# Gate product from one float32 copy, compressed scores block-diagonal, leftovers of tile 1 behind the output of tile 0, first query panel in halves

## The chip, the cores and the metric

The kernel runs on one core of one Trainium2 chip. The metric is the device time of one execution in microseconds (us), the median of several runs; lower is better. TensorE is PE in the profile, VectorE DVE, ScalarE ACT, GpSimd POOL and SyncE SP.

## What is computed

Four transformer layers on 256 tokens of width 1024, all in float32. The change touches the third layer (native sparse attention, NSA) and the router of its expert layer.

```
proj = x @ w_in
gates = jax.nn.sigmoid(proj[..., ATTN_WIDTH + 6 * kvd:])   # 48 columns
k_cmp = compress_blocks(rope(kv[:, :, 0]), ...)            # 15 blocks of 32 tokens per group
p_c = masked_softmax(q @ k_cmp, cmp_end <= t)              # compressed branch
# selected and window branches: ordinary causal attention at 256 tokens
out = gate0 * o_c + gate1 * o_s + gate2 * o_w              # then @ w_out, + h, rms_norm
```

16 heads of 64 share 4 groups of keys. The expert layer takes, for each token, 8 heads of 256 query columns; each half of a head's query (128 columns) is scored against 128 keys, the 16 best of each half give 256 sums, and the 16 best of these name 16 of 16384 experts. With 8 x 16 = 128 experts a token it forms `h = gelu(u[e] . x)` and adds `gate * h * v[e]`. The fourth layer is forgetful attention and another such expert layer.

## The kernel before, in words

Tokens lie on the 128 partitions in two tiles (0 and 1). Matrices come as panels of 2 MB (1024 x 512) through a ring of two slots; SyncE issues their loads.

**Front, 0 to 840 us.** Two layers and the wide NSA product. Here a float32 product is done as three fp32r products: ScalarE casts a high part of each panel (`ring_hi`), VectorE forms the rest (`ring_lo`), and the transposed tokens have the same two parts (`xT`, `xT_lo`). `evict_turned` (ScalarE) copies the transposed tokens out of PSUM banks 4 to 7, VectorE's `lower_turned` subtracts. After the last wide panel, `narrow` (line 686) multiplies the tokens by the 48 gate columns: for each tile, each of 8 slices and each of the two parts one float32 matmul, with the tokens as weights.

**Middle, from 840 us.** `MIDDLE` is an order written out by hand. Each name is one step that fills one PSUM bank, on six rotating banks; PE runs the names in order, and ScalarE or VectorE (`by_dve`) empties each bank in the same order. A and B are transposes of the queries of tiles 0 and 1, T and D and E of key twins (D1, E1 those of tile 1), H the compression's hidden product (four panels), G and C its further steps, c0 and c1 the compressed scores (line 1006), X and e0 to e3 the compressed values (e2, e3 for tile 1), S, P, O the scores, the turned shares and the values of one batch of four heads of tile 0; o turns the mixed result and u0, u1 multiply it by the output matrix. Names with ! fill no bank (!E exponentials of a batch, !m !x !n the compressed softmax). For c0 and c1, each of 16 (tile, head pair) has one matmul on the 64 rows of one head with 16 columns; c0 does the first heads of the pairs, c1 the second.

After u1, VectorE adds both halves to h and runs `norm_late` (ScalarE's `root` gives the square root); xn of tile 0 is then ready.

**route00.** The router of tile 0, also in order: y0, y1 turn xn; w0 to w3 multiply it by the four query panels (`project_late`, line 872), W turns four blocks of 128 query columns, s scores them against the keys (line 895). ScalarE copies each result. One panel holds two heads. VectorE ranks head 0 (`rank_head`), then `choose` writes the experts of piece 0 (head 0 alone), then it computes the gates of the piece, for which it waits for ScalarE's exponentials (g0, after s1 in ScalarE's order), then it ranks head 1, and only then does it begin the expert slots.

**Expert stream, to the end.** 4 windows of 128 slots. GpSimd gathers, for each slot, 128 rows of u and of v (0.52 MB each, line 2118), four u slots ahead of four v slots, in rings of eight rows; it waits for a free slot (`u_used`, `v_used`). VectorE forms the dot with u (line 1757), ScalarE the gate and a diagonal matrix, PE adds diagonal x v into PSUM (line 852). Four slots are one tick, and between ticks each engine runs the steps of NSA tile 1, of the routers and of the last layer that are due (`STAGES`).

Of the kernel before, what the change touches and what calls it, by code (L numbers as in the profile page):

```python
# [17 lines left out]
F32 = mybir.dt.float32  # L18
# [6 lines left out]
P = 128  # L25
SEQ = 256
# [48 lines left out]
def in_batch(kind, t, b):  # L75
# [11 lines left out]
          ["G2", "c0", "c1", "S4a", "S4b", "P3a", "O2", "!m", "!E4", "!x", "G3"],  # L87
# [3 lines left out]
          ["P7a", "O6", "D1", "E1"],  # L91
          ["O7", "e2", "e3"],
          ["o0", "o1"], ["u0", "u1"]]
# [12 lines left out]
def fox_plan(t):  # L106
    plan = [(1, ["x0", "x1"]), (2, ["f", "q0"]), (3, ["q1", "Q0"]), (4, ["c", "k0", "Q1"]),
            (5, ["k1", "K0"]), (6, ["v0", "K1"]), (7, ["v1"])]
    for i in range(BATCHES + 2):
# [10 lines left out]
          ("route00", -1, [(0, ["y0", "y1", "w0", "W0", "s0", "w1", "w2", "W1", "s1", "w3", "W2", "s2", "W3", "s3"])]),  # L120
# [12 lines left out]
WEIGHTS = {"w": 0, "q": 0, "k": 2, "v": 4, "u": 6}  # L133
USES = [key for key in ORDER if key[1][0] in WEIGHTS or key[1][0] == "H"]
# [153 lines left out]
def build(nc, x, panels, gains, consts, line_consts, rel_bias, lam, subln, small, fbias, keys, u0, v0, u1, v1, out,  # L288
          probe=None):
    lines_dram = nc.dram_tensor("bias_lines", (HEADS, P, LINE), F32).ap()  # L290
    with ExitStack() as ctx:
# [93 lines left out]
        kcT = z(GROUPS, CW)  # L385
# [44 lines left out]
        tokT = o[:, 1, :].rearrange("p (a b) -> p a b", a=KT)  # L430
        turned_q = [o[:, 1, :].rearrange("p (a b) -> p a b", a=PAIRS),
# [53 lines left out]
        gate_logits = sem("gate_logits")  # L485
        gate_exps_ready = sem("gate_exps_ready")
# [93 lines left out]
        @block.sync  # L580
        def _(sp):
            sp.dma_start(h[:, :, :], x.rearrange("(t p) d -> p t d", p=P)).then_inc(first_loaded, 16)

            sp.wait_ge(first_loaded, 16 * 5)
            for s in range(2):
                if s == 1:
                    sp.wait_ge(landed[0], 16)
                sp.dma_start(ring[:, s, :], panels[s]).then_inc(landed[s], 16)
            pairs = N_PANELS // 2
            with sp.Fori(1, pairs) as i:  # L590
                for s in range(2):

                    sp.wait_ge(panel_used, i * 2 + (s - 1))
                    sp.dma_start(ring[:, s, :], panels[i * 2 + s]).then_inc(landed[s], 16)
            for n in range(2 * pairs, N_PANELS):
                sp.wait_ge(panel_used, n - 1)
                sp.dma_start(ring[:, n % 2, :], panels[n]).then_inc(landed[n % 2], 16)
            for i, key in enumerate(USES):
                n = N_PANELS + i
                if i < 2:  # L600
                    sp.wait_ge(panel_used, n - 1)
                else:
                    filled(sp, USES[i - 2])
# [8 lines left out]
        def _(pe):  # L612
# [68 lines left out]
            def narrow(w, cols):  # L681

                for t in range(TILES):
# [191 lines left out]
            def route(stage, layer, t, begin, plan):  # L875
                for tick, names in plan:
                    yield begin + tick
                    for name in names:
                        key = stage, name
                        if name[0] == "y":  # L880
                            pe.wait_ge(xn_ready, NORM_NUMBER[("nsa", "ffn1")[layer], t])
                            turn_half(key, xn[:, t, :])
                        elif name[0] == "w":
                            emptied(pe, (stage, "y1"))
                            project_late(key)
                        elif name[0] == "W":
                            i = int(name[1])
                            turn_projected(key, wqT[:, 4 * i:4 * i + 4, :])
                        else:
                            i = int(name[1])  # L890
                            emptied(pe, (stage, f"W{i}"))
                            pe.wait_ge(keys_landed, 16 * (TILES * layer + t + 1))
                            to = bank(key)
                            for j in range(4):
                                last = mm(to[:, j * P:(j + 1) * P], wqT[:, 4 * i + j, :], keysT[:, 4 * i + j, :],
                                          start=True, stop=True)
                            last.then_inc(bank_filled, 1)
# [56 lines left out]
            def middle(stage, begin, plan):  # L954
                pe.wait_ge(proj_read, 2 * AHEAD + 2 * done)
                for tick, names in plan:
                    yield begin + tick
                    for name in names:
# [40 lines left out]
                        elif kind == "c":  # L999
                            emptied(pe, (stage, "B1"))  # L1000
                            emptied(pe, (stage, "C0"))
                            to, own = bank(key), slice(i * HD, (i + 1) * HD)
# [124 lines left out]
        def _(act):  # L1127
# [17 lines left out]
            def evict_turned(call):  # L1145
# [4 lines left out]
                for t in range(TILES):  # L1150
# [4 lines left out]
                    if t == 0:  # L1155
                        upper(first, 0, steps=range(early, CHUNKS))

# [137 lines left out]
            def route(stage, layer, t, begin, plan):  # L1295
                moments = [(begin + tick + (begin + tick >= 0), names) for tick, names in plan]
                if stage == "route00":
                    names = plan[0][1]
                    moments = [(begin, names[:9] + ["g0"] + names[9:])]
                moments += [(chosen_at(stage, begin, piece), [f"g{piece}"])  # L1300
                            for piece in range(stage == "route00", len(CHOSEN[TILES * layer + t]))]
                for tick, names in sorted(moments, key=lambda m: m[0]):
                    yield tick
                    for name in names:
# [6 lines left out]
                        if name[0] == "y":  # L1311
                            copy_bank(key, tokT[:, 4 * i:4 * i + 4, :], fours(key))
                        elif name[0] in "wW":
# [28 lines left out]
            def middle(stage, begin, plan):  # L1342
# [28 lines left out]
                root()  # L1371
# [102 lines left out]
        def _(dve):  # L1474
# [312 lines left out]
            def route(stage, layer, t, begin, plan):  # L1787
                window = TILES * layer + t
                for head in range(P_HEADS):
                    yield ranked_at(stage, begin, head)  # L1790
                    emptied(dve, (stage, f"s{head // 2}"))
# [79 lines left out]
            def middle(stage, begin, plan):  # L1871
# [3 lines left out]
                v.memset(hidT, 0.0)  # L1875
                dve.wait_ge(gate_exps_ready, 1)
# [4 lines left out]
                for tick, names in plan:  # L1881
                    yield begin + tick
                    for name in names:
# [20 lines left out]
                        elif name == "C0":  # L1904
                            filled(dve, key)
                            v.tensor_copy(kcT, shadow_bank(key)[:, 0:GROUPS * CW].rearrange("p (a b) -> p a b", a=GROUPS))\
                                .then_inc(dve_emptied, 1)
# [9 lines left out]
                        elif kind == "c":  # L1917
                            filled(dve, key)
                            for t in range(TILES):
                                last = v.scalar_tensor_tensor(  # L1920
                                    out=over(cmp_s[:, t, i, :], [[2 * CW, PAIRS], [1, CW]]),
                                    in0=over(shadow_bank(key)[:, t * PAIRS * CW:], [[CW, PAIRS], [1, CW]]), scalar=SCALE,
                                    in1=over(const("cbias")[:, t * CW:(t + 1) * CW], [[0, PAIRS], [1, CW]]),
                                    op0=ALU.mult, op1=ALU.add)
# [21 lines left out]
                dve.drain()  # L1946
                norm_late(0, "ffn0", xn_ready)
# [287 lines left out]
```

## Time and profile before

| What | us |
|---|---|
| median of 3 runs | 2611.57 (2604.69 to 2615.46) |
| the profiled execution | 2603.34 |
| its span in the trace | 2601.2 |
| PE busy | 2196.6 (84%) |
| VectorE busy | 1408.9 (54%) |
| GpSimd busy | 1139.3 (44%) |
| ScalarE busy | 873.8 (34%) |

### The profile page before, as it was taken

How to read it: one execution, taken by the hardware profiler on the slowest of the kernel's cores; microseconds unless marked ns; L12 is line 12 of the kernel's file. 1: busy time of each engine (PE TensorE's matmuls, PEld its weight loads, DVE VectorE, ACT ScalarE, POOL GpSimd, SP SyncE). 2: the span in 40 equal slices, each digit the busy share in tenths (PEclk: the TensorE clock that was granted, in tenths of full speed). 3: DMA queues.
4: the chain of work that ended last, by engine and by line, in shares of the span. 5: the costliest groups of instructions: out<-in, count | busy, mean ns of one | idle time of the engine just before them, and what ended most of it. 6: DMA issues, size and time to landing. Idle time of an engine off the chain costs nothing.

```text
span 2601.2 us, 24135 instructions
## 1 busy us (share of the span) xinstructions
PE 2196.6 (84%) x7346; PEld 1283.3 (49%) x7346; DVE 1408.9 (54%) x2912; ACT 873.8 (34%) x2112; POOL 1139.3 (44%) x1075
## 2 busy tenths in 40 slices
PE   5879999889989987688896989798899897767767
PEld 4656876668868743254342444343345343323222
DVE  2365445364457347855565654465665457664433
ACT  2344443444533423254222324222235222222121
POOL 0000000000000006667666757667666767777674
PEclk8899999899999888888998999898999998888888
DMA  8504544225444339889999999999999999999997
GB/s 229 190 25 153 194 182 150 105 81 190 174 168 151 148 114 390 321 306 333 414 414 381 368 412 371 391 413 407 372 414 348 404 412 359 355 372 380 363 369 282
DMA packets 165575, 754.64 MB, mean 290 GB/s; under 512 B 18320, under 2 KB 18464, under 8 KB 152544
## 3 DMA queue, kind: packets, MB, share of 16 engines
q0 software_dynamic: 149168, 544.02, 55.1%
q1 hardware_dynamic: 13952, 197.14, 19.6%
q10 hardware_dynamic: 2352, 12.24, 1.2%
q8 instruction: 48, 0.79, 0.1%
q14 instruction: 55, 0.45, 0.0%
HBM read 749.13 MB, written 4.19 MB: 290 GB/s over the span
## 4 chain that ended last, share of the span: by engine, by line
PE 37%; DVE 15%; POOL 12%; issue 10%; DMA 9%; another core or an unknown queue 6%; ACT 3%; DVEq 1%; ACTq 0%; POOLq 0%; SPq 0%
POOL Z L2118 12%; PE ps L852 9%; DMA Z<-v,experts 6%; PE ps L639 6%; PE ps L641 6%; PE ps L640 6%; DVE Z L1757 6%; PE ps L872 3%; DMA Z<-u,experts 2%; PE ps L978 1%; PE ps L913 1%; DMA ring<-panels 1%; PE ps L904 1%; DVE ring_lo L1606 1%
## 5 line engine op out<-in xcount | busy, mean ns | idle before, releaser
L852 PE MATMUL ps<-Z 128*128 128x512 f32 x2048 | 1014.7, 652 | 254.0 <-DMA Z<-v,experts 174.3
L852 PEld LDWEIGHTS ps<-Z 128*128 128x128 f32 x2048 | 416.6, 209 | 814.9 <-issue 569.3
L1757 DVE CUSTOM_DVE_ANT_0 Z<-Z,xn 128x1024 f32<-128x1024 f32 x512 | 609.2, 1224 | 297.8 <-DMA Z<-u,experts 235.0
L2118 POOL DMA_INDIRECT Z<-u,experts x512 | 571.5, 1116 | 388.8 <-issue 161.2
L2118 POOL DMA_INDIRECT Z<-v,experts x512 | 543.8, 1062 | 219.8 <-issue 134.3
L1606 DVE TENSOR_TENSOR ring_lo<-ring,ring_hi 128x1024 fp32r<-128x1024 f32 x212 | 246.0, 1219 | 274.8 <-ACT ring_hi L1142 274.8
L639 PE MATMUL ps<-ring_hi,xT_lo 128*128 128x512 f32 x592 | 238.1, 402 | 32.5 <-DVE xT_lo L1654 17.8
L872 PE MATMUL ps<-ring,o 128*128 128x512 f32 x576 | 255.0, 596 | 1.9 <-ACT o L1278 1.4
L1142 ACT CAST ring_hi<-ring 128x1024 fp32r<-128x1024 f32 x212 | 206.9, 1049 | 129.2 <-DMA ring<-panels 119.6
L641 PE MATMUL ps<-ring_hi,xT 128*128 128x512 f32 x592 | 232.9, 393 | 0.0
L640 PE MATMUL ps<-ring_lo,xT 128*128 128x512 f32 x592 | 232.9, 393 | 0.0
L1259 ACT ACTIVATE hdot<-hdot 128x4 f32<-128x4 f32 x128 | 26.4, 206 | 557.7 <-DVE hdot L1757 389.6
L2107 POOL COPY Z<-pj 128x256 f32 x16 | 6.4, 400 | 434.3 <-ACTq L526 343.3
L1270 ACT ACTIVATE Z<-cst,wslot 128x128 f32<-128x128 f32 x512 | 164.7, 390 | 66.7 <-remote 29.0
L872 PEld LDWEIGHTS ps<-ring,o 128*128 128x128 f32 x576 | 108.8, 191 | 133.6 <-issue 131.6
L2150 POOL COPY ksc<-pj 128x512 f32<-128x512 f32 x5 | 3.4, 710 | 332.5 <-DVE pj L1676 319.3
L639 PEld LDWEIGHTS ps<-ring_hi,xT_lo 128*128 128x128 f32 x592 | 113.0, 191 | 62.5 <-DVE ring_lo L1606 16.0
L640 PEld LDWEIGHTS ps<-ring_lo,xT 128*128 128x128 f32 x592 | 113.0, 191 | 24.0 <-issue 1.2
L641 PEld LDWEIGHTS ps<-ring_hi,xT 128*128 128x128 f32 x592 | 112.5, 190 | 24.1
L1264 ACT ACTIVATE wslot<-hdot,gate_w 128x1 f32<-128x1 f32 x512 | 109.6, 284 | 9.1 <-issue 0.3
L639 PE MATMUL ps<-ring_hi,hT 128*128 128x512 f32 x256 | 101.2, 395 | 5.3 <-DVE hT L1614 5.3
L1278 ACT COPY scratch<-ps 128x512 f32<-128x512 f32 x68 | 38.0, 577 | 189.4 <-PE ps L872 71.9
(257 smaller groups left out, 2067.1 us busy)
## 6 DMA issues: line engine op xcount, KB each, us to landing
ring<-panels SPq DMA_DIRECT2D x93, 2048.0 KB
Z<-u,experts POOLq DMA_INDIRECT x512
Z<-v,experts POOLq DMA_INDIRECT x512
gain<-gains ACTq DMA_DIRECT2D x4, 1024.0 KB, 7.7
pj<-keys ACTq DMA_DIRECT2D x4, 1024.0 KB
bias_lines<-xn POOLq DMA_DIRECT2D x1, 3072.0 KB, 38.5
gain<-gains ACTq DMA_DIRECT2D x5, 512.0 KB, 6.2
Z<-bias_lines POOLq DMA_DIRECT2D x1, 2048.0 KB, 9.5
```

The source lines that it names most:

```text
L639: mm(out, b, c, start=start, stop=False)
L640: mm(out, a, d, start=False, stop=False)
L641: return mm(out, a, c, start=False, stop=stop)
L852: last = mm(ps[:, c, :], diag[s], vrow[s][:, c * NC:(c + 1) * NC], start=slot == 0, stop=slot == SLOTS - 1)
L872: last = mm(to, tokT[:, k, :], w[:, k * NC:(k + 1) * NC], start=k == 0, stop=k == KT - 1)
L1142: copy(ring_hi[:, slot, c * CH:(c + 1) * CH], ring[:, slot, c * CH:(c + 1) * CH]).then_inc(hi_ready, 1)
L1264: f(own[:, s:s + 1], cols[:, s:s + 1], ACT.Copy, scale=gate_w[:, t, slot + s:slot + s + 1])
L1270: f(diag[n % RING], ident, ACT.Copy, scale=own[:, s:s + 1]).then_inc(diag_ready, 1)
L1278: copy(to, src).then_inc(act_emptied, 1)
L1606: v.tensor_tensor(ring_lo[:, slot, at], ring[:, slot, at], ring_hi[:, slot, at].bitcast(F32), ALU.subtract).then_inc(lo_ready, 1)
L1757: v.tensor_tensor_reduce(out=urow[s], in0=urow[s], in1=xn[:, t, :], scale=1.0, scalar=0.0, op0=ALU.mult, op1=ALU.add, accum_out=hdot[:, t, ...
L2118: g.indirect_dma_start(out=rows[s], out_offset=None, in_=tables[layer], in_offset=bass.IndirectOffsetOnAxis(ap=experts[:, t, slot:slot + 1 ...
```

## The change

Four edits.

1. `evict_turned` copies, before the NSA product, all transposed tokens once more out of PSUM as plain float32 (`xT_all`, in the place of `o`, four copies of 128x512); `narrow` waits for them and does one matmul per tile and slice instead of two.
2. The compressed keys are stored block-diagonal (`kcT` gets a second half, cleared by a memset; C0 copies two quadrants). c0 does both heads of a pair in one matmul over all 128 rows with 32 columns; c1 is gone, and VectorE reads 256 elements a tile at once.
3. e2, e3, D1 and E1 (tile 1) move behind u0, u1 and the norm of tile 0, which now has a name of its own, !r.
4. In route00, w0, W0 and s0 become i0, j0, t0 (head 0: 256 columns, two transposes, two score products) and i1, j1, t1 (head 1). Both use the one panel; the slot is given free after i1. VectorE waits for t0 and t1.

```diff
           ["H3", "S3a", "S3b", "P2a", "O1", "!E3"],
-          ["G2", "c0", "c1", "S4a", "S4b", "P3a", "O2", "!m", "!E4", "!x", "G3"],
+          ["G2", "c0", "S4a", "S4b", "P3a", "O2", "!m", "!E4", "!x", "G3"],
...
-          ["P7a", "O6", "D1", "E1"],
-          ["O7", "e2", "e3"],
-          ["o0", "o1"], ["u0", "u1"]]
+          ["P7a", "O6"], ["O7"],
+          ["o0", "o1"], ["u0", "u1", "!r"], ["e2", "e3", "D1", "E1"]]
...
-          ("route00", -1, [(0, ["y0", "y1", "w0", "W0", "s0", "w1", "w2", "W1", "s1", "w3", "W2", "s2", "W3", "s3"])]),
+          ("route00", -1, [(0, ["y0", "y1", "i0", "j0", "t0", "i1", "j1", "t1", "w1", "w2", "W1", "s1", "w3", "W2", "s2", "W3", "s3"])]),
...
-USES = [key for key in ORDER if key[1][0] in WEIGHTS or key[1][0] == "H"]
+USES = [key for key in ORDER if key[1][0] in "wqkvuH" or key[1] == "i0"]
+LAST_USE = {("route00", "i0"): ("route00", "i1")}
...
-                        for n, a in enumerate(tokens(k, t)):
-                            last = mm(ps[:, 4 + t, 0:cols], a.bitcast(F32), w[:, k * cols:(k + 1) * cols],
-                                      start=k == 0 and n == 0, stop=k == KT - 1 and n == 1)
+                        last = mm(ps[:, 4 + t, 0:cols], xT_all[:, k, t * P:(t + 1) * P], w[:, k * cols:(k + 1) * cols],
+                                  start=k == 0, stop=k == KT - 1)
...
+                        elif name[0] == "i":
+                            emptied(pe, (stage, "y1"))
+                            w, b, to = late_panel((stage, "i0")), int(name[1]), bank(key)
+                            for k in range(KT):
+                                at = k * NC + b * NC // 2
+                                last = mm(to[:, 0:NC // 2], tokT[:, k, :], w[:, at:at + NC // 2], start=k == 0, stop=k == KT - 1)
+                            last.then_inc(bank_filled, 1)
+                        elif name[0] == "j":
+                            b = int(name[1])
+                            emptied(pe, (stage, f"i{b}"))
+                            to = bank(key)
+                            for j in range(2):
+                                last = tr(to[:, j * P:(j + 1) * P], wqT[:, 2 * b + j, :], ident)
+                            last.then_inc(bank_filled, 1)
...
-                                    at = (t * PAIRS + pair) * CW
-                                    last = mm(to[:, at:at + CW], turned_q[t][own, pair, :], kcT[own, pair // 2, :],
+                                    at = (t * PAIRS + pair) * 2 * CW
+                                    last = mm(to[:, at:at + 2 * CW], turned_q[t][:, pair, :], kcT[:, pair // 2, :, :],
...
+                if NEXT[call] == "nsa":
+                    act.wait_ge(xt_ready, 2 * TILES * (call + 1))
+                    for t in range(TILES):
+                        for b in range(2):
+                            last = copy(xT_all[:, 4 * b:4 * b + 4, t * P:(t + 1) * P],
+                                        ps[:, 4 + 2 * t + b, :].rearrange("p (a b) -> p a b", a=4))
+                    last.then_inc(xt_all_ready, 1)
...
+                v.memset(kcT, 0.0)
```

## Rows read from the trace of the kernel before

**Rows 1.** windows: stretch, length, busy us by engine, PE clock, DMA share, GB/s

```profile
979.90:2575.61 1595.71, 1317.74 (x3362) 606.64 (x3360) 938.12 (x2227) 473.32 (x1471) 1111.69 (x1021) 0.91 0.98 378
...
996.84:1077.00 80.16, 57.56 (x119) 25.09 (x119) 69.76 (x229) 22.19 (x70) 61.48 (x55) 0.82 1.02 406
```

**Rows 2.** timeline of GpSimd: start, length, what, idle before and its releaser

```profile
979.90 1.02 POOL L2118 DMA_INDIRECT Z<-u,experts  x1 [123.64 <-DVE experts L1730]
...
998.85 1.18 POOL L2118 DMA_INDIRECT Z<-u,experts  x1 [4.22 <-DVE hdot L1757]
...
1083.65 1.18 POOL L2118 DMA_INDIRECT Z<-u,experts  x1 [5.61 <-DVE hdot L1757]
```

**Rows 3.** timeline of VectorE, first rank, gate norm, first dot

```profile
969.50 0.49 DVE L1682 MAX8 ranks<-ksc 128x8 f32<-128x128 f32 x2 [15.44 <-ACT ksc L1278]
...
987.08 0.17 DVE L1743 TENSOR_REDUCE ranks<-ranks 128x1 f32<-128x16 f32 x1 [7.14 <-ACT ranks L1293]
...
996.84 1.23 DVE L1757 CUSTOM_DVE_ANT_0 Z<-Z,xn 128x1024 f32<-128x1024 f32 x1 [1.25 <-issue]
```

**Rows 4.** timeline of ScalarE, copy of s1

```profile
984.94 0.59 ACT L1278 COPY ksc<-ps 128x512 f32<-128x512 f32 x1 [1.25 <-PE ps L895]
```

**Rows 5.** windows of the gate product alone (line 686)

```profile
840.15:844.10 3.95, 3.95 (x37) 3.95 (x36) 1.00 0.69 218
...
844.75:849.80 5.05, 5.05 (x25) 5.05 (x25) 0.50 0.72 296
```

**Rows 6.** chain of waits, by time: start, length, what

```profile
850.07 5.76 PE ps L951 x32
...
855.83 7.02 PE ps L978 x32
...
871.77 0.87 PE ps L951 x8
...
909.67 1.12 PE ps L904 x4
...
910.78 1.61 PE ps L913 x8
```

**Rows 7.** timeline of VectorE, last memset and the adds of T0 to T3

```profile
845.32 0.17 DVE L1875 MEMSET Z<- 128x128 f32 x1
...
852.70 5.39 DVE L1889 TENSOR_TENSOR Z<-ps,smallw 64x480 f32<-64x480 f32 x8 [1.27 <-PE ps L951]
```

**Rows 8.** timeline of ScalarE and VectorE, split of the second NSA panel

```profile
790.53 3.91 ACT L1142 CAST ring_hi<-ring 128x1024 fp32r<-128x1024 f32 x4
...
791.63 4.63 DVE L1606 TENSOR_TENSOR ring_lo<-ring,ring_hi 128x1024 fp32r<-128x1024 f32 x4 [0.63 <-ACT ring_hi L1142]
...
796.98 0.59 ACT L1168 COPY pj<-ps 128x512 f32 x1 [2.54 <-PE ps L641]
```

**Rows 9.** windows of the compressed scores alone (line 1006)

```profile
892.76:895.50 2.74, 2.74 (x25) 2.74 (x25) 1.00 0.99 425
...
896.95:902.20 5.25, 5.25 (x28) 5.25 (x28) 0.50 0.01 3
```

**Rows 10.** timeline of VectorE, adds of O6 and O7

```profile
929.95 0.18 DVE L1825 RECIPROCAL shares<-totals 128x4 f32<-128x4 f32 x1 [1.60 <-PE ps L913]
...
932.16 0.86 DVE L1837 SCALAR_TENSOR_TENSOR o<-ps,shares,o 128x64 f32<-128x64 f32 x4
```

**Rows 11.** timeline of PE: y0 and y1, w0, w1 and w2

```profile
954.11 1.97 PE L859 MATMUL ps<-cst,xn 128*128 128x128 f32 x8 [5.10 <-DVE xn L1783]
...
956.76 8.91 PE L872 MATMUL ps<-ring,o 128*128 128x512 f32 x16 [0.68 <-ACT o L1278]
...
968.68 13.90 PE L872 MATMUL ps<-ring,o 128*128 128x512 f32 x32
```

**Rows 12.** timeline of SyncE, load of the panel for w3

```profile
975.74 0.33 SPq L604 DMA_DIRECT2D ring<-panels  x1
```

**Rows 13.** windows, a stretch of the first attention

```profile
158.00:160.00 2.00, 0.39 (x1) 0.30 (x2) 1.70 (x4) 0.36 (x1) 0.00 (x0) 1.00 0.00 0
```

More of the change, by code:

```diff
@@ L384, in build @@
         cmp_s = z(TILES, HEADS, CW)
-        kcT = z(GROUPS, CW)
+        kcT = z(GROUPS, 2, CW)
         bd = z(2, 8, HD)
@@ L602, in _ @@
                 else:
-                    filled(sp, USES[i - 2])
+                    filled(sp, LAST_USE.get(USES[i - 2], USES[i - 2]))
                 sp.dma_start(ring[:, n % 2, :], panels[panel_source(key)]).then_inc(landed[n % 2], 16)
@@ L889, in route @@
                         else:
-                            i = int(name[1])
-                            emptied(pe, (stage, f"W{i}"))
+                            i, blocks, turned = int(name[1]), *((2, "j") if name[0] == "t" else (4, "W"))
+                            emptied(pe, (stage, f"{turned}{i}"))
                             pe.wait_ge(keys_landed, 16 * (TILES * layer + t + 1))
                             to = bank(key)
-                            for j in range(4):
-                                last = mm(to[:, j * P:(j + 1) * P], wqT[:, 4 * i + j, :], keysT[:, 4 * i + j, :],
+                            for j in range(blocks):
+                                last = mm(to[:, j * P:(j + 1) * P], wqT[:, blocks * i + j, :], keysT[:, blocks * i + j, :],
                                           start=True, stop=True)
@@ L1312, in route @@
                             copy_bank(key, tokT[:, 4 * i:4 * i + 4, :], fours(key))
+                        elif name[0] in "ijt":
+                            to = (ksc if name[0] == "t" else wqT)[:, 2 * i:2 * i + 2, :]
+                            copy_bank(key, to, fours(key)[:, 0:2, :])
                         elif name[0] in "wW":
@@ L1370, in middle @@
                             soft_exps(stage, int(name[2]))
-                root()
+                        elif name == "!r":
+                            root()
             def nsa(stage, begin, plan):
@@ L1790, in route @@
                     yield ranked_at(stage, begin, head)
-                    emptied(dve, (stage, f"s{head // 2}"))
+                    emptied(dve, (stage, f"t{head}" if stage == "route00" and head < 2 else f"s{head // 2}"))
                     rank_head(head, ksc[:, 2 * head:2 * head + 2, :])
@@ L1905, in middle @@
                             filled(dve, key)
-                            v.tensor_copy(kcT, shadow_bank(key)[:, 0:GROUPS * CW].rearrange("p (a b) -> p a b", a=GROUPS))\
-                                .then_inc(dve_emptied, 1)
+                            for m in range(2):
+                                own = slice(m * HD, (m + 1) * HD)
+                                last = v.tensor_copy(kcT[own, :, m, :], shadow_bank(key)[own, 0:GROUPS * CW]
+                                                     .rearrange("p (a b) -> p a b", a=GROUPS))
+                            last.then_inc(dve_emptied, 1)
                         elif name == "C1":
@@ L1920, in middle @@
                                 last = v.scalar_tensor_tensor(
[L1921 to L1923 removed]
+                                    out=cmp_s[:, t], in0=over(shadow_bank(key)[:, t * HEADS * CW:], [[CW, HEADS], [1, CW]]),
+                                    scalar=SCALE,
+                                    in1=over(const("cbias")[:, t * CW:(t + 1) * CW], [[0, HEADS], [1, CW]]),
                                     op0=ALU.mult, op1=ALU.add)
```

15 lines of the change are left out of this document (10 added, 5 removed).

## The prediction

> **What bounds the kernel now.** I read the page's forty slices and queue table first, then windows from the first gather on, then GpSimd's timeline, then the chain of waits through the stretch before it. From 980 us on the kernel streams expert rows, and everything else lies beside that: the DMA engines are 0.98 busy over 1596 us [rows 1]. Their bytes don't change, so the end comes earlier only as far as the stream starts earlier. When does it really start? GpSimd issues its first gather at 979.90, twelve in all (eight u, four v), and stands until VectorE's first dot frees a u slot [rows 2]. That dot runs at 996.84. VectorE had ranked head 0 from 969.50, then sat 7.14 us for the gate exponentials of piece 0, and ranked head 1 [rows 3]. The exponentials were late because ScalarE runs them in order behind the copy of s1, which ended at 985.5 [rows 4]. From 996.84 to 1077 VectorE is busy 69.8 of 80.2 us, and at 1083.65 GpSimd waits on it for 5.6 us [rows 1, 2]: VectorE's clock from the first dot, not the first gather, sets the pace. So I follow what moves the first dot: the chain 840 to 955 (PE almost throughout), then route00.
>
> **Gate product.** Each float32 matmul appears as two records in the trace (the product's 32 matmuls are 64 records). After: 16 matmuls, 32 records. The rate was 3.95/36 = 0.11 us a record at the full clock and 5.05/25 = 0.20 once the granted clock had fallen to half (1.2 GHz) at 844.3 [rows 5]. 32 x 0.11 = 3.5 us, so the product ends near 843.8 instead of 850.07: 6.3 us. The 32 transposes behind it took 5.76 us, largely at half clock; eight of B0 and B1 took 0.87 at the full one, so 3.5 for 32 [rows 6]. They would end at 847.3, but H0 needs T0 from VectorE. That engine ends its memsets at 845.5, gets one more (0.17, the size of the last of them), then adds and inverts the gates (about 1.1 with its waits) and does T0's two adds (2 x 5.39/8 = 1.35): 848.2 [rows 7]. H0 began at 855.8, so the gain is 7.5, with VectorE late next. If the clock falls all the same behind the product, the transposes keep 5.76: 849.5, gain 6.3. If everything runs at half clock, 32 x 0.20 + 5.76 leaves 3. I take 7.5: the clock fell 4.15 us into the product, and this one lasts 3.5.
>
> The price is ScalarE's four copies (128x512, 0.55 us each, 2.2) before the dense product, behind VectorE's last xT_lo at 791.0. They hold back the split of the second panel: ScalarE began it at 790.53 and VectorE its first quarter at 791.63; now 793.8 and 794.9, first quarter done at 796.1. PE wants it when the first panel is through, just before 796.98 [rows 8]. Hidden by 0.4 us; if that cover is gone it costs up to 1. TensorE's new wait is satisfied 40 us early.
>
> **Compressed scores.** c0 and c1 were 32 matmuls of 16 columns on 64 rows: 64 records, 892.8 to 902.3, 2.74 us for 25 at full clock and 5.25 for 28 at half [rows 9]. Now 16 matmuls of 32 columns on 128 rows, 32 records. No row has that shape; the nearest, 48 columns on 128 rows, costs 0.11 [rows 5], the half-clock price 0.20. So 3.5 to 6.5 us against 9.5: gain 6.0 down to 3.0. I take 3.5. Behind it runs a loop of transposes, values, VectorE's add, ScalarE's exponentials: at half clock 1.1 and 1.6 on PE [rows 6], and about 0.95 and 1.7 on the two others, a period of some 5.4 us. In the likeliest case it stays at half clock (these columns are narrower than the gate's, and waits follow), and the gain is 6.2 with small waits saved. If the clock stays up, P (four transposes, half of 0.87, and 0.15 for the way out) and O (8 records of 0.11) are together some 1.2 us shorter: 1.8 until P4a, then 0.9, 0.1 (there VectorE is the bound, with the compressed softmax) and 1.1 in the further rounds, together 9.9 with the 6.0. VectorE's reads of the product keep their elements, and the second kcT copy (0.2) lies 9 us before its use.
>
> **Leftovers.** e2, e3 (4 records of 13.90/32 = 0.43 [rows 11], 1.75) and D1, E1 (0.87) leave the stretch between P7a and o0. Not all of it is gained: O7 moves up by D1's and E1's 0.87, but VectorE's adds for O6, from 929.95, and for O7 follow each other in 1.35 each; they then end at 932.65, where they ended at 933.02 [rows 10]. Gain 0.4; 0 if the share copy for O7 is late, and 2.6 would be the whole of it. They land behind u1, where PE idled 5.10 us for the norm [rows 11]: 2.6 of work hides in it. ScalarE's two copies (1.1) come behind the root and before y0. VectorE's copies of e2 and e3 come behind the norm, where it waited 15.44 us [rows 3]; i0 and j0 take their banks, and the copies are through a little before i0. If they were not, i0 would wait up to 0.7.
> That leaves 2.5 us of idle PE where 5.1 had been. After 5.1 the clock was at half: y0 and y1 took 1.97 and w0 8.91 against 13.90 for two panels [rows 11]. Kept at full, y0 and y1 are 0.9 to 1.0 shorter: 0.9; 0 if the clock falls.
>
> **Query panel in halves.** Before: w0 8.91 us, then copy, W0, copy, s0, copy; head 0 ranked at w0's start + 12.7, first gather at + 23.1. After: i0 is 16 records of 256 columns; H0's 32 of that width took 7.02 [rows 6], so 3.5. Then copies of half the width (0.35), two transposes (0.3), two score matmuls (0.6): with releases 2.3 instead of 3.8. Head 0 starts at + 5.8, first gather + 16.3: 6.9 us earlier relative to the panel. But VectorE blocks at the gate norm until ScalarE has passed s1. Until there PE has i0, j0, t0 5.3, i1, j1, t1 5.3, w1 and w2 14.0 (13.90 before), W1 and s1, so s1's copy ends at + 27.6 where it was + 28.8. The exponentials follow by 1.5 and the first dot 9.8 after them: + 39.0 instead of + 40.1 [rows 3, 4, 11]. So this edit moves the first gather by 6.9 and the first dot by 1.1. The stretch between is a longer wait on VectorE, about 13 us instead of 7.14. The panel for w2 is issued when i1 is filled, + 8.9, as before when w0 was; the one for w3 when w1 is filled, now behind the first gathers; before, at 975.74, ahead of them [rows 12]. If the clock falls before i0 as it did before w0, i0 takes 1.8 more and this term is -0.7.
>
> **Sum.** 7.5 + 6.2 + 0.4 + 0.9 + 1.1 = 16.1 us, first dot at 980.7, and the stream behind it is rigid. The profiled execution took 2603.3 (span 2601.2); 2587.2 for it. It lies 8.2 under the median shown, 2611.57; I set the change against the median: 2595.5, say 2596.
>
> **A rule of the Trainium skill.** TensorE's clock rose again at about 854.6, inside a run of nothing but transposes that had begun at 850.07 [rows 5, 6]. The Trainium skill's page "TensorE: Matmul & The Clock Gate", Part 4 (PE-mode transpose), says that transposes don't count as busy time for the clock. By that, the transposes behind the gate product would lower the clock rather than hold it, and the gate term would be 6.3, the sum 14.9. The row speaks against the rule; I give it weight only within rival B.
>
> **Rivals.** Those on the clock differ in where it falls.
> A. It stays up through the scores too: gate 7.5, scores 9.9, rest 2.4: 19.8, time 2592. For it: in the first attention, with the same mixture of small transposes and products, PE was busy only 0.39 of 2 us in one stretch and the clock stayed 1.00 [rows 13]. Against: it had fallen 2.7 us into the old scores, with PE busy throughout.
> B. It falls at the old places and also before i0: 6.3 + 4.5 (between 3.0 and 6.0) + 0.4, y as before, and i0 some 1.8 longer, which leaves -0.7 there: 10.5, time 2601. For it: the clock fell 4.15 and 2.7 us into the narrow products, and neither new one is much shorter. The transpose rule of the Trainium skill pulls this way.
> C. The head start carries: DMA is full from 980 on [rows 1], so twelve gathers served 6.9 - 1.1 = 5.8 us sooner would shorten the end as well: 16.1 + 5.8 = 21.9, time 2590. Against: only eight u slots exist, the twelve (12 x 0.524 MB at 406 GB/s) take 15.5 us, and then DMA has nothing until the first dot.
> D. The other side: w3's panel starves. It is issued 1.4 us after the first gather, behind 12 x 0.52 MB; before, it was issued 4.2 us ahead of it [rows 2, 12]. PE, in order, stands at w3, ScalarE behind it can't make a diag, v slots don't come free and GpSimd stops. In fair sharing it lands at + 30, 3 us late, without effect. It costs from + 43 on, us for us: w3 7, W3 and s3 3, gates and diags 3, first v slot 2 make + 58, and GpSimd restarts at + 41 with twelve gathers, some 17 us, before it asks for a v slot; from + 59 it eats all 16 us, and if gathers keep it back until their second round of eight is in (another 11 us a round), the kernel is slower than before, 2615 to 2630. Against: later panels are issued in the full stream and the stream goes on.
> E. The change does not do what it says: the stream re-times itself and swallows the gain, its clock being 0.91 on average, 0.82 at first [rows 1]: 2606 to 2614.
>
> **Chances.** Forecast 0.45 (own range 11 to 21 us less: 2591 to 2601), A 0.17, B 0.19, C 0.07, D 0.05, E 0.07. About 0.5% (13 us, below 2598.5) can be told from no change. Faster: 0.45 x 0.75 + 0.17 x 0.95 + 0.19 x 0.25 + 0.07 = 0.61; slower: most of D, 0.04; same 0.35. The range takes in A, B and C and part of E, and runs of before are spread over 11 us: 2585 to 2609.
>
> **What would show it.** Product over 32 records of 0.11 and H0 near 848; c0 near 885 over 3.5 us; u0 near 921; e2 to E1 right behind u1; first gather near 958, then a wait of some 13 us on VectorE and the first dot near 981; DMA share below 1 between them. Wrong if the first dot moves by under 10 us, if the stream from first dot to end (1604 us) lengthens, or if PE waits for the second panel of the dense product.

## The result

The changed kernel takes 2580.89 us (median of 13 runs, 2575.39 to 2594.56); the kernel before, run beside it, took 2597.62 (13 runs, 2576.61 to 2615.46). The ratio is 0.9941, 95% interval [0.9919, 0.9964]: 0.6% faster. The difference was forecast at 16.1 us and came out at 16.7 by the medians, 15.3 by the ratio. The absolute time was forecast at 2596 and lies 15 us lower, below the range (2585): it had been set on a median of 2611.57, and the same kernel then gave 2597.62.

Where the time came from is seen in the profile of the changed kernel. Its windows show the gate product alone (the answer to [rows 5]; PE and weight load busy, clock, DMA share, GB/s):

```profile
837.40:842.00 4.60, 3.67 (x32) 3.56 (x32) 1.00 0.74 241
```

32 records instead of 64, all at 1.00. The timeline of PE, from there to route00 (answers to [rows 6, 9, 11]):

```profile
837.47 3.67 PE L688 MATMUL ps<-smallw,o 128*128 128x48 f32 x32
840.97 1.06 PE L967 MATMUL ps<-cst,pj 128*128 128x128 f32 x8
841.86 1.91 PE L967 MATMUL ps<-cst,ksc 128*128 128x128 f32 x16
843.61 1.04 PE L967 MATMUL ps<-cst,ranks 128*128 128x128 f32 x8
...
845.41 0.81 PE L994 MATMUL ps<-ring,Z 128*32 128x256 f32 x3 [0.77 <-DVE Z L1918]
...
882.39 1.97 PE L1022 MATMUL ps<-Z,o 128*128 128x32 f32 x16
884.20 2.79 PE L1022 MATMUL ps<-Z,pj 128*128 128x32 f32 x16
886.91 1.23 PE L943 MATMUL ps<-gain,o 64*128 64x128 f32 x8
...
918.34 14.00 PE L874 MATMUL ps<-ring,o 128*128 128x512 f32 x32 [0.73 <-ACT o L1301]
932.17 1.88 PE L1032 MATMUL ps<-Z 128*128 128x512 f32 x4
...
937.44 1.09 PE L861 MATMUL ps<-cst,xn 128*128 128x128 f32 x8 [2.51 <-DVE xn L1811]
939.63 5.41 PE L890 MATMUL ps<-ring,o 128*128 128x256 f32 x16 [1.10 <-ACT o L1301]
```

H0 begins 7.94 us behind the start of the gate product, where it began 15.6 behind it [rows 5, 6], and what it waits for is VectorE's T0 (0.77). c0 takes 4.52 us: its first 16 records took 1.97, the next 16, mostly at half clock, 2.79. The leftovers stand behind u1, PE then waits 2.51 for the norm instead of 5.10 [rows 11], and i0 takes 5.41 for 16 records, where 3.5 was forecast. On VectorE, the waits for head 0, for the gate norm, and the first dot (answers to [rows 3]):

```profile
947.56 0.49 DVE L1710 MAX8 ranks<-ksc 128x8 f32<-128x128 f32 x2 [8.61 <-ACT ksc L1301]
...
970.88 0.17 DVE L1771 TENSOR_REDUCE ranks<-ranks 128x1 f32<-128x16 f32 x1 [12.87 <-ACT ranks L1316]
...
977.99 1.23 DVE L1785 CUSTOM_DVE_ANT_0 Z<-Z,xn 128x1024 f32<-128x1024 f32 x1
```

And GpSimd (answers to [rows 2]), the first gather and the first one that needs a dot:

```profile
957.98 1.03 POOL L2151 DMA_INDIRECT Z<-u,experts  x1 [112.89 <-DVE experts L1758]
...
980.00 1.18 POOL L2151 DMA_INDIRECT Z<-u,experts  x1 [7.28 <-DVE hdot L1785]
```

The first gather is 21.9 us earlier than before, the first dot 18.9. Of both, 2.7 us is no part of the change: the gate product itself began at 837.47 in this execution, at 840.15 before. It is 49.10 us from the first record of the dense product to the gate product in both profiles, without a wait of PE for the second panel, so the price of ScalarE's four copies did not come. From the first dot to the end it is 1601 us, against 1604 before (answer to [rows 1]; busy PE, weight load, VectorE, ScalarE, GpSimd, then clock, DMA share, GB/s):

```profile
960.50:980.00 19.50, 17.32 (x66) 9.43 (x64) 8.18 (x34) 5.30 (x9) 9.40 (x11) 1.00 1.02 425
977.99:2578.80 1600.81, 1317.66 (x3346) 603.66 (x3343) 935.97 (x2205) 474.33 (x1475) 1112.81 (x1012) 0.91 0.97 375
```

### The profile page after: what moved, and what is told of

Read it like the earlier page. It is cut to its first block, busy times and chain, and to the rows that moved or that the text cites. A ratio compares the mean times of both kernels' runs of the same rounds, so it can differ in the third digit from the quotient of the medians.

```text
span 2578.8 us, 24047 instructions
## 1 busy us (share of the span) xinstructions
PE 2174.9 (84%) x7298; PEld 1267.5 (49%) x7298; DVE 1408.5 (55%) x2912; ACT 877.5 (34%) x2119; POOL 1148.3 (45%) x1075
## 4 chain that ended last, share of the span: by engine, by line
PE 42%; POOL 13%; DVE 12%; DMA 10%; issue 9%; another core or an unknown queue 4%; ACT 2%; DVEq 1%; ACTq 0%; POOLq 0%; SPq 0%
POOL Z L2151 13%; PE ps L854 12%; DMA Z<-v,experts 8%; PE ps L641 6%; PE ps L642 6%; PE ps L643 6%; PE ps L874 5%; DVE Z L1785 4%; DMA Z<-u,experts 1%; DMA ring<-panels 1%; PE ps L994 1%; PE ps L929 1%; PE ps L920 1%; DVE ring_lo L1634 1%
## 5 line engine op out<-in xcount | busy, mean ns | idle before, releaser
L2151 POOL DMA_INDIRECT Z<-u,experts x512 | 564.4, 1102 | 361.9 <-issue 156.9
L2151 POOL DMA_INDIRECT Z<-v,experts x512 | 559.8, 1093 | 229.0 <-issue 143.4
L874 PE MATMUL ps<-ring,o 128*128 128x512 f32 x560 | 246.0, 593 | 0.7 <-ACT o L1301 0.7
L1301 ACT COPY scratch<-ps 128x512 f32<-128x512 f32 (+1 forms) x70 | 38.3, 567 | 188.2 <-PE ps L874 60.0
```

The source lines that it names most:

```text
L874: last = mm(to, tokT[:, k, :], w[:, k * NC:(k + 1) * NC], start=k == 0, stop=k == KT - 1)
L1301: copy(to, src).then_inc(act_emptied, 1)
L2151: g.indirect_dma_start(out=rows[s], out_offset=None, in_=tables[layer], in_offset=bass.IndirectOffsetOnAxis(ap=experts[:, t, slot:slot + 1 ...
```

## The experiments

For each run the table gives the start of some steps, in us behind the first record of the gate product (differences of timeline rows; 840.15 for the kernel before). "panel" is the duration of the first late product (w0, or the half i0). The ratio is to the kernel before on the same chip, whose median stands behind it. A filler is a 128x512 product with zeros whose result nobody reads.

| kernel | H0 | S4a | y0 | panel | first gather | first dot | ratio | before, us |
|---|---|---|---|---|---|---|---|---|
| before, as shown | 15.6 | 62.1 | 114.0 | 8.9 | 139.8 | 156.7 | | |
| before, once more | 12.3 | 60.0 | 111.8 | 9.4 | 138.1 | 153.9 | | 2595.76 |
| changed, as shown | 7.9 | 49.4 | 100.0 | 5.4 | 120.5 | 140.5 | 0.9941 | 2597.62 |
| changed, second | 8.0 | 48.7 | 102.9 | 6.0 | 124.3 | 144.3 | 0.9963 | 2595.76 |
| changed, third | 8.8 | 50.8 | 102.9 | 5.6 | 124.1 | 144.1 | 0.9939 | 2619.77 |
| gate alone | 7.7 | 53.6 | 105.4 | 9.6 | 131.9 | 146.2 | 0.9975 | 2527.58 |
| scores alone | 15.6 | 57.1 | 108.2 | 10.1 | 135.2 | 149.5 | 0.9971 | 2527.58 |
| order alone | 12.3 | 59.8 | 112.7 | 9.1 | 138.7 | 153.1 | 0.9997 | 2527.58 |
| halves alone | 14.0 | 60.2 | 112.0 | 6.0 | 133.3 | 153.4 | 1.0012 | 2527.58 |
| g0 early | 8.5 | 49.1 | 102.6 | 6.5 | 124.2 | 131.8 | 0.9983 | 2595.76 |
| fillers everywhere | 8.1 | 53.8 | 105.4 | 3.7 | 124.3 | 144.3 | 0.9964 | 2595.76 |
| filler in the hole | 7.9 | 50.0 | 101.9 | 3.7 | 120.8 | 140.8 | 0.9959 | 2525.87 |
| three edits | 8.1 | 48.9 | 102.2 | 9.9 | 128.5 | 142.9 | 0.9959 | 2525.87 |
| three and filler | 7.8 | 48.5 | 100.2 | 7.1 | 123.8 | 138.2 | 0.9948 | 2525.87 |
| the same again | 8.8 | 50.8 | 102.8 | 7.1 | 126.4 | 143.7 | 0.9925 | 2619.77 |
| late | 8.0 | 49.6 | 113.7 | 3.7 | 132.5 | 152.5 | 0.9992 | 2619.77 |

**One edit at a time.** The gate product from one copy:

```diff
-                        for n, a in enumerate(tokens(k, t)):
+                        last = mm(ps[:, 4 + t, 0:cols], xT_all[:, k, t * P:(t + 1) * P], ...
...
```

> The kernel before with the gate product from one float32 copy alone. Theory (each edit moves the first dot by its own piece of the chain, and the stream behind is rigid): product over in 3.7 us instead of 9.8, H0 7.7 us sooner after the product's start, first dot and end 7.7 us sooner: ratio 0.997. Rival (the stream re-times itself and swallows the gain): H0 7.7 us sooner, ratio 1.000. If ScalarE's four copies held back the second panel, the product would begin up to 1 us later after the last turn of the tokens.

Measured 2523.38 us, 0.9975 [0.9961, 0.9989], the first dot 7.7 earlier than in the repeat of the kernel before; 4.6 of that stand at H0, 1.8 more came where the clock in c0 and c1 fell later, and 1.4 is a wait of VectorE that only the repeat had. The compressed scores block-diagonal:

```diff
-          ["G2", "c0", "c1", "S4a", ...
+          ["G2", "c0", "S4a", ...
```

> The kernel before with block-diagonal compressed scores alone. Theory: c0 takes 4.5 us (clock falls inside it) instead of 9.5, the loop behind stays at half clock, P4a and the end 5.8 us sooner: ratio 0.998. If the clock stays up through the loop (rival A of the prediction): 9.9 us, ratio 0.996. If c0 is wholly at half clock: 3 us.

Measured 2522.14, 0.9971 [0.9956, 0.9986]. From c0 to S4a it is 4.5 us, against 9.5 and 10.7 in the two profiles of the kernel before: 5 to 6.2. The leftovers moved:

```diff
-          ["P7a", "O6", "D1", "E1"],
-          ["O7", "e2", "e3"],
+          ["P7a", "O6"], ["O7"],
...
```

> The kernel before with e2, e3, D1, E1 behind the norm alone. Theory: o0 0.4 to 0.7 us sooner, y0 and y1 0.5 shorter if the clock stays up, w0 still partly at half clock; first dot 1 to 2 us sooner, ratio 0.9995. Rival (all 2.6 us of moved work come off the path): ratio 0.999, not to be told apart by time, but by the start of o0 in the trace.

Measured 2527.07, 0.9997 [0.9985, 1.0009]: nothing that can be measured. The timelines show a loss that the prediction did not have. In the old order PE comes to o0 and o1 without a wait; with D1, E1, e2 and e3 gone from there, it waits 1.70 us for VectorE, and u0 and u1 then begin at half clock. First the kernel before, then the changed kernel's third profile:

```profile
933.25 1.04 PE L859 MATMUL ps<-cst,o 128*128 128x128 f32 x8
935.01 14.00 PE L872 MATMUL ps<-ring,o 128*128 128x512 f32 x32 [0.73 <-ACT o L1278]
```

```profile
920.58 1.09 PE L861 MATMUL ps<-cst,o 128*128 128x128 f32 x8 [1.70 <-DVE o L1865]
922.40 15.70 PE L874 MATMUL ps<-ring,o 128*128 128x512 f32 x32 [0.73 <-ACT o L1301]
```

Here, with the leftovers alone moved, u0 and u1 took 15.70 too: 0.6 us won up to o0, 1.7 lost behind it. Of the eleven profiles in the new order nine show such a loss, 1.6 to 3.1 us; of the five in the old order none does. The changed kernel's first profile is one of the two without it. A product with zeros in that wait was not tried. The first query panel in halves:

```diff
-"y0", "y1", "w0", "W0", "s0", "w1", ...
+"y0", "y1", "i0", "j0", "t0", "i1", "j1", "t1", "w1", ...
```

> The kernel before with the first query panel in halves alone. Theory (the first dot sets the pace, and it hangs on the copy of s1): first gather 5 to 7 us sooner after y0, s1's copy 0 to 1 us later, first dot within 1 us of where it was, ratio 1.000. Rival C (the head start carries): end 5 to 7 us sooner, ratio 0.9975. Open: after shows no wait of VectorE for instructions in the rank of head 1 (2.8 us before); if that belongs to this edit, the first dot comes 2 to 3 us sooner.

Measured 2529.84, 1.0012 [0.9999, 1.0024]. The first gather is 26.3 us after y0 in the repeat of the kernel before, 21.4 here, and the time doesn't follow it; rival C falls. Two edits make the gain; the product of the four ratios is 0.9955.

**The whole again.**

> The kernel before, unchanged, for a second trace. Theory (the time before is a matter of the chip, and the prediction's absolute time missed by the base it started from): first dot 156 to 157 us after the gate product's start less the 2.8 us in which VectorE waited for instructions there, so 153.5 to 157, and the stream behind it another length than 1604 us if the chip is another. Rival (the missed base is noise between executions on one chip): stream within 5 us of 1604.

> The changed kernel, unchanged, beside the kernel before on one chip. Theory: gate 7.7 + scores 5.8 + order 0.5 to 1.2 + halves 0 = 14 to 15 us, ratio 0.9943 at a base of 2530, first dot 13 to 16 us sooner after the product's start. Rival (the four help each other, as 22 us between the two first profiles suggest): ratio 0.992 or less.

The kernel before, in the one execution that was traced again, gave 2590.87, with 1597 us behind its first dot; the changed one 2587.67 (12 runs), 0.9963 [0.9940, 0.9987]. And on a further chip:

> The changed kernel once more, beside the next two on one chip. The forecast's difference to the kernel before is 16 us: a ratio of 0.9936 to 0.9950 whichever the chip, where the absolute time may be 2510 or 2580 (the kernel before gave 2527.6, 2525.9 and 2595.8 on three chips). If the ratio here is 0.9965 or more, the gain at the first dot isn't all kept.

2604.86 against 2619.77, 0.9939 [0.9914, 0.9964]. The mean of the three is 0.9948, 13.6 us of 2600. The kernel before has had medians of 2597.62, 2595.76, 2619.77 and 2527.58, 2525.87, by the chip. Where the 70 us lie is seen in the windows from the first dot to the end of one and the same program (the last kernel below, three edits and filler), first on a chip of the slower sort, then on one of the faster:

```profile
982.60:2583.40 1600.80, 1309.08 (x3354) 600.87 (x3354) 936.75 (x2205) 473.53 (x1476) 1105.15 (x1012) 0.92 0.97 375
```

```profile
974.74:2504.10 1529.36, 1296.29 (x3345) 596.32 (x3343) 938.77 (x2205) 472.30 (x1475) 1094.68 (x1013) 0.93 1.00 393
```

VectorE and ScalarE are busy equally long; the DMA engines moved 375 GB/s on the one chip and 393 on the other. 1600.80 x 375 and 1529.36 x 393 make 600 and 601 MB, the same bytes. Why one chip moves them more slowly is open.

**Is the first dot what counts?** Gates of piece 0 right behind t1, ahead of w1, instead of behind s1:

```diff
-                    at = names.index("s1") + 1
+                    at = names.index("t1") + 1
```

> The changed kernel with the gate exponentials of piece 0 (g0) in ScalarE's order behind t1 instead of behind s1. Theory (the head start of the first gathers is lost because VectorE waits for g0): VectorE's wait at the gate norm falls from 13 to about 2 us, the first dot comes 10 to 12 us sooner, GpSimd restarts as much sooner, then meets the first v slot, whose release stands behind w3 and s3: 4 to 11 us remain at the end, ratio to before 0.990 to 0.9925. Rival (the DMA engines, full from the first gather on, set the pace already): first dot sooner, end unchanged against the changed kernel, 0.994.

Measured 2591.73, 0.9983 [0.9958, 1.0008]. The first dot came 12.5 us sooner than in the changed kernel's second profile and the time did not: the changed kernel's ratio on this chip is 0.9963. VectorE's timeline of this kernel (the gate norm, then the second and the fourth dot) and GpSimd's:

```profile
960.61 0.17 DVE L1771 TENSOR_REDUCE ranks<-ranks 128x1 f32<-128x16 f32 x1 [0.28 <-ACT ranks L1316]
...
971.43 1.23 DVE L1785 CUSTOM_DVE_ANT_0 Z<-Z,xn 128x1024 f32<-128x1024 f32 x1 [2.29 <-DMA Z<-u,experts]
...
978.27 1.23 DVE L1785 CUSTOM_DVE_ANT_0 Z<-Z,xn 128x1024 f32<-128x1024 f32 x1 [4.34 <-DMA Z<-u,experts]
```

```profile
985.78 0.93 POOL L2151 DMA_INDIRECT Z<-v,experts  x1 [0.31 <-issue]
990.69 1.18 POOL L2151 DMA_INDIRECT Z<-u,experts  x1 [3.98 <-DVE hdot L1785]
```

VectorE's wait for the gates is gone. In its place it waits 2.29 and 4.34 us for gathered rows, and then 3.3 us for nothing that the profile shows; the fifth dot leads by 2.7 us only. s3 is copied at 154.9 behind the gate product instead of 146.9. At the 13th gather the lead over the changed kernel is 6.1 us, at the 25th 2.6, and at the 81st it is 1.6 behind. Its windows and, below them, the changed kernel's (second profile):

```profile
1010.00:1070.00 60.00, 42.71 (x92) 17.88 (x92) 50.77 (x164) 12.96 (x46) 45.90 (x42) 0.91 1.01 394
1070.00:1090.00 20.00, 13.16 (x34) 6.25 (x33) 18.68 (x29) 8.14 (x23) 10.38 (x9) 0.76 0.62 217
```

```profile
1010.00:1070.00 60.00, 46.49 (x94) 19.46 (x95) 54.78 (x184) 14.64 (x53) 47.51 (x42) 0.86 1.00 382
1070.00:1090.00 20.00, 10.67 (x31) 5.40 (x31) 18.68 (x29) 8.11 (x23) 13.13 (x12) 0.77 0.82 288
```

So 9.8 of the 12.5 us were gone by the fifth dot, 6.6 of them because the rows had not landed. Until 1070 DMA is full in both; then DMA stands at 0.62 beside a VectorE that is busy 18.68 of 20. What took the rest, this or the later s3, was not tried apart.

The opposite, a first dot that is only made later, by 19 products with zeros ahead of y0:

```diff
                            nsa_out(key)
+                        if name == "E1":
+                            filler(19)      # mm(ps, zero, const("upto")), 128x512
```

> The changed kernel with nineteen 128x512 products with zeros behind E1 in place of none: 17.9 us of TensorE (1.88 us a pair in the test before), of which 2.5 us fit into the wait for the norm, so the first half panel, the first gather and the first dot come 15.4 us later (17 less 2 that the clock gives back in i0 if it counts), and nothing else is touched. Theory R (the stream behind the first dot is rigid): the time is 13.5 to 15.5 us over the changed kernel's, a ratio between the two of 1.0055 to 1.006, and the kernel before, whose first dot is 16 us later than the changed one's, is its equal (ratio to before 0.9995 to 1.0005). Rival E (the stream re-times and swallows part of a lead): the first dot is 13.5 to 15.5 us later and the end less than 8 us.

```profile
934.51 16.47 PE L972 MATMUL ps<-cst,zero 128*128 128x512 f32 x38
950.82 1.04 PE L861 MATMUL ps<-cst,xn 128*128 128x128 f32 x8
952.96 3.72 PE L890 MATMUL ps<-ring,o 128*128 128x256 f32 x16 [1.10 <-ACT o L1307]
```

The delay was smaller than I had meant: u0 fell out 1.7 us shorter in this profile, the fillers took 16.5, i0 won 1.9 from the full clock, and the first dot is 8.4 us later than in the changed kernel beside it. The time is 9.6 us longer by the medians (2614.45), 13.9 by the two ratios (0.9992 [0.9964, 1.0020] and 0.9939): no sign that the shift is swallowed, though the two intervals together leave some 10 us either way, more than the shift itself, so this run alone does not show it. All runs but g0 early together: a straight line of (ratio - 1) x median of before against the first dot's distance from 153.9, thirteen ratios weighted by their intervals, has a slope of 1.02 with a standard error of 0.12, and 0.6 +/- 1.0 at zero. The points scatter 1.3 times as widely as their intervals say, and each first dot is from one execution, where that of the same kernel moves by up to 5.5 us; the error is therefore rather 0.16 or more. One us at the first dot is about one us at the end, within the 16 us that these edits span.

**Clock at the first half panel.** Products with zeros in c0, in the loop and in the wait before y0:

```diff
+                            filler(1)       # behind each half of c0, before P4a to P7a
...
+                            filler(2)       # behind E1
```

> The changed kernel with added products of zeros (128x512, two records each, results never read): one behind each half of c0, one ahead of P4a, P5a, P6a and P7a, two behind E1. It asks what the half clock costs from c0 to i0. Theory: the clock stays at full, the loop's rounds are 0.9 to 1.2 us shorter, e0 and e1 1.75, i0 1.9, against 1.75 us for the two in c0: first dot 3 to 5 us sooner than in the changed kernel, ratio to before 0.9925. Rival: the added work is in the way (each ahead of a P can delay it by up to 0.9) and the clock falls all the same: 2 to 4 us later, ratio 0.9955.

Measured 2582.66, 0.9964 [0.9939, 0.9990]. i0 took 3.72 instead of 5.96, but S4a came 5 us later; the first dot stayed. The clock fell in c0 all the same and was at half up to 904, so neither what I had expected nor its rival came. So only the two behind E1:

> The changed kernel with two 128x512 products with zeros behind E1, in the stretch in which TensorE waits for the norm before y0; nothing else is added (the test before it had products in c0 and in the loop too). Theory K (the half clock on i0 is what that wait leaves behind): i0 takes 3.7 us in place of 5.4 to 6.0, o0 and u0 stand where they stood, the first gather comes 1.7 to 2.3 us sooner behind y0, and the first dot as much, with a ratio to the changed kernel of 0.9993. Rival (the first dot waits for the second half and its copies, which TensorE gives at full clock either way): i0 is faster, the first gather is sooner, and the first dot is where it was within 0.5 us, no change in time.

Measured 2516.22, 0.9959 [0.9945, 0.9973]. In the timeline of PE:

```profile
940.75 1.88 PE L972 MATMUL ps<-cst,zero 128*128 128x512 f32 x4
943.43 1.09 PE L861 MATMUL ps<-cst,xn 128*128 128x128 f32 x8 [0.80 <-DVE xn L1817]
945.62 3.72 PE L890 MATMUL ps<-ring,o 128*128 128x256 f32 x16 [1.10 <-ACT o L1307]
```

From y0 to the first dot it is 38.9 us, against 40.6, 41.4 and 41.2 in the three profiles of the changed kernel. The fillers cost nothing where PE waits anyway, and bring about 2 us at the first dot. In the time that is below what can be told.

**Without the halves.**

```diff
-"i0", "j0", "t0", "i1", "j1", "t1",
+"w0", "W0", "s0",
```

> The change without its fourth edit: gate product, block-diagonal scores and moved leftovers, first query panel whole. Theory T (the halves bring the first gather forward and the first dot not, and cost up to 0.1%): the first gather 5 us later behind y0 than with the halves, the first dot at the same distance from y0 within 1 us, and a ratio to the kernel before of 0.994 (0.9975 x 0.9971 x 0.9997 = 0.9943), no worse than the whole change on the same chip. Rival H (the halves bring something once the other three are in): the first dot is 2 us or more further behind y0 than in the whole change, and the ratio is 0.9955 or more.

Measured 2515.34, 0.9959 [0.9943, 0.9975]; from y0 to the first dot 40.7, no more than with the halves. Then both:

> Three edits (without the halves) and the two products with zeros behind E1. If the clock at the first late panel is a cost of its own: w0 takes 7.0 us in place of 8.9 to 10.1, the first gather and the first dot come 2 to 3 us sooner behind y0 than in the kernel with three edits alone, and the ratio to the kernel before is 0.993, the best of all versions. If the first dot is held by something else, the dot doesn't move and the ratio is that of the three edits, 0.994.

```profile
934.15 1.88 PE L957 MATMUL ps<-cst,zero 128*128 128x512 f32 x4
936.83 1.10 PE L860 MATMUL ps<-cst,xn 128*128 128x128 f32 x8 [0.80 <-DVE xn L1798]
939.03 7.13 PE L873 MATMUL ps<-ring,o 128*128 128x512 f32 x16 [1.10 <-ACT o L1292]
```

w0 takes 7.13 us, where it took 9.90 in the three edits alone, and y0 to the first dot 37.9. Measured 2512.92, 0.9948 [0.9929, 0.9968]; and once more, beside the changed kernel:

> Three edits without the halves, with two products with zeros in the wait before y0, once more, to compare with the changed kernel on the same chip. Its first dot was 37.9 us behind y0, the changed kernel's 40.6 to 41.4. If that is kept: 2.5 to 3 us under the changed kernel, a ratio to before 0.001 lower; if the stream takes it: equal within 0.0005.

2596.95 (10 runs), 0.9925 [0.9891, 0.9960], against 0.9939 for the changed kernel. From y0 to the first dot it was 40.9 this time, 3.2 of them VectorE's waits for nothing that the profile shows. Both comparisons point to the fastest version of all, three edits and two products with zeros, but the intervals overlap: it isn't shown that it beats the changed kernel. It does beat the kernel before.

## Why the prediction was right and where it was wrong

- **Gate product, 7.5.** H0 came 7.7 us sooner in the pair of profiles, with VectorE next, as worked out. But 7.5 was counted against one execution: in kernels without this edit H0 stood at 15.6, 15.6, 12.3, 12.3 and 14.0. With the edit it is 7.7 to 8.8. The term is 3.5 to 7.9, the forecast its upper part. The clock fell 4.2 to 6.7 us into the old product, by the execution, and not always at the 4.15 that the forecast went by. (With everything at half clock its own numbers leave 3.5, not 3.)
- **Scores, 6.2.** 5.0 at S4a, 5.8 at P4a. c0 took 4.5, not 3.5, and 3.7 and 5.0 in the two further profiles; all stood between my bounds of 3.5 and 6.5. The clock fell 2.7, 3.6 and 2.2 us into it, and the loop stayed at half: the likeliest case; rival A is false.
- **Leftovers 0.4, y 0.9.** o0 gained 0.5 in the first profile. y0 and y1 took 1.09 there, as at full clock, but half of that went to the copy before i0 (PE idle 1.10 instead of 0.68), and then the clock fell before i0: rival B's last part. i0 took 1.9 more. In the second and third profile y0 and y1 took 1.80 and 1.97, as before, and u0 and u1 lost 2.2 and 1.7 at half clock. The sum had no term for that: it took the 2.6 us of leftovers out from ahead of o0 without asking what the clock does in the wait that they leave. Over the executions these two terms are nothing or less.
- **Halves, 1.1.** None: 1.0012 alone. The mechanism was right (first gather early, then 12.87 us at the gate norm, 13 forecast), the small rest did not show. From y0 to the first dot, VectorE's waits for nothing shown left out, it is 40.0 to 41.3 us in the six profiles with the whole panel and no filler, 40.6 to 41.4 in the four with halves and the gates where they were: the prediction's own other case (the clock falls before i0, -0.7) lies nearer.
- **The sum came out all the same, 16.2 us behind the gate product, and that is luck.** The shown profile of the kernel before held 2.8 us of VectorE waits for nothing that the profile shows ahead of its first dot (one is the 1.25 in [rows 3]); nothing ties them to the change: from the gate norm to the first dot it took 9.8 us, 8.6 in its repeat, 7.1 in the changed kernel, and 10.1 in one run of three edits and filler. Against the repeat the changed kernel's three profiles gain 13.4, 9.6 and 9.8, and the three ratios say 13.6. The first profile also had the full clock in u0 and u1 that the two others lacked. The forecast difference was some 2.5 us too large, inside two of three intervals.
- **Between first gather and first dot DMA was to be below 1.** It was 1.02 in the first profile: w3's 2 MB are served there too, which the forecast had left out of its case against rival C. Rival D, where that panel starves, did not come: w3 began at 968.54, right behind s1 and without a wait, and the stream after it is as long as before. Rival E is false by the slope of 1.
- **The failed step** is "It lies 8.2 under the median shown, 2611.57; I set the change against the median: 2595.5". What the runs showed in its place is a base of 2597.62: three runs had the median 2611.57, thirteen with these three among them 2597.62, and by chip it goes from 2526 to 2620. From 2597.62 the same 16.1 give 2581.5, measured 2580.89. The profiled execution (2603.34, giving 2587.2) was nearer, but still 6 us too high. A range for the absolute time had to hold the base's own uncertainty, at least 14 us here; mine held 11 us of spread and spent the rest on the rivals. Within the difference, the terms that failed are the leftovers and the halves, as above.

The Trainium skill's "TensorE: Matmul & The Clock Gate", Part 4 (PE-mode transpose), would have let the clock fall behind the shorter gate product. The 32 transposes behind it took from 840.97 to 844.65, 0.11 us each, as at full clock. In the changed kernel's third profile the clock did fall there, 3.6 us behind the product's start, at its end, but it rose again 3.4 us later, with only transposes in between. These traces do not bear the rule out.

## What to carry to other kernels

Follow the time to the one event behind which the rest is rigid, and check that by moving the event alone in both directions: over thirteen kernels the end followed it about one to one, but 12.5 us earlier by that event alone was not kept, because another limit stood close behind. Give a forecast as a difference and keep the base's uncertainty apart; take steps at a changing clock from more than one profile before they become a term. Work that is moved off the path may have been what kept the clock up for the next product: look at the wait that it leaves. Where PE waits anyway ahead of a long product, a product with zeros in the wait costs nothing and can save the clock.

## What the runs showed of the hardware

- The same program (three edits and filler) moved 393 GB/s behind its first dot on one chip and 375 on another, 2513 us against 2597.
- Narrow products with PE wholly busy did not hold the clock: c0, 128x32, was at 1.00 until 885 and then at half with no gap before (1.97 and 2.79 us for 16 records each). The same program lost it at another place in another execution: 2.2 to 3.6 us into c0, 4.2 and 6.4 us into the old gate product. Idle of 2.5 us and eight transposes ahead of i0 gave 5.4 to 6.5 us for it in four profiles; with products with zeros in that wait it took 3.72 in all three. Idle of 1.7 to 1.8 us and eight transposes ahead of u0 left it at half clock at first in nine of eleven profiles.
- VectorE can stand 1.2 to 1.8 us for nothing that the profile shows, in one execution and not in the next, at the same place (1.53 and 1.25 us in the kernel before, 1.51 and none in its repeat).
